# Two attentions on TensorE: the values of the item two back move ahead of the turns of the last item

## The reference

```python
s_w = jnp.einsum("bqgrd,bkgd->bgrqk", qb, kw) * scale
p_w = masked_softmax(s_w, mask_w)
o_w = jnp.einsum("bgrqk,bkgd->bqgrd", p_w, vw)
...
o = gb[..., 0:1] * o_c + gb[..., 1:2] * o_s + gb[..., 2:3] * o_w
```

```python
sc = (jnp.einsum('bchd,bicjhd->bhcij', q_row, k_win).astype(jnp.float32)
      + bias.astype(jnp.float32)[None])
p = jax.nn.softmax(sc.reshape(bsz, nh, GRID_W, win_r * NA_WIN_COLS), axis=-1)
...
return jnp.einsum('bhcij,bicjhd->bchd', p, v_win)
```

## Time and profile before

| what | value |
|---|---|
| median of 3 runs | 1695.55 us (1694.1 to 1696.63) |
| the profiled execution | 1696.4 us |
| its span, first to last instruction | 1694.7 us |
| mean granted TensorE clock | 0.999 |
| TensorE busy | 1661.1 us (98%) |
| DVE, ACT, POOL busy | 616.4, 664.9, 736.8 us |

### The profile page before, as it was taken

The page is one execution under the profiler, slowest core; times in us unless marked ns, Lnnn a source line. Parts: engine busy times, 40 slices in busy tenths (PEclk is TensorE's granted clock), DMA queues, the critical chain, the costliest instruction groups (busy, mean ns, idle before and its releaser), DMA issues. The chain is left out here.

```text
span 1694.7 us, 23049 instructions
## 1 busy us (share of the span) xinstructions
PE 1661.1 (98%) x8890; PEld 1335.7 (79%) x8890; DVE 616.4 (36%) x1156; ACT 664.9 (39%) x1013; POOL 736.8 (43%) x639
## 2 busy tenths in 40 slices
PE   9999999999999999999999999999999999999999
PEld 7777778877779888888878786767788888888887
DVE  5431865433242111011147343544556331212131
ACT  5223577454353432212245434434553441323130
POOL 5223343463144444644525544333355354544543
PEclk9999999999999999999999999999999999999999
DMA  5243101441033243433222234212264223232321
GB/s 181 75 149 97 63 29 55 143 142 58 26 99 100 76 124 100 145 96 82 99 77 75 100 108 141 85 56 90 68 210 161 86 81 110 83 100 99 100 100 50
DMA packets 152945, 166.09 MB, mean 98 GB/s; under 512 B 11959, under 2 KB 114434, under 8 KB 152835
## 3 DMA queue, kind: packets, MB, share of 16 engines
q1 hardware_dynamic: 145232, 151.20, 27.8%
q10 hardware_dynamic: 7602, 13.41, 2.2%
HBM read 155.68 MB, written 9.30 MB: 97 GB/s over the span
## 5 line engine op out<-in xcount | busy, mean ns | idle before, releaser
L807 POOL TENSOR_TENSOR w_low<-raw,w_high 128x512 fp32r<-128x512 f32 x501 | 668.5, 1368 | 845.1 <-ACT w_high L952 844.5
L952 ACT CAST w_high<-raw 128x2048 fp32r<-128x2048 f32 x127 | 239.0, 1882 | 234.0 <-PE bank L2321 221.1
L2326 PE MATMUL bank<-xT_high,w_high 128*128 128x512 f32 (+1 forms) x672 | 248.2, 375 | 0.0
L2327 PE MATMUL bank<-xT_low,w_high 128*128 128x512 f32 (+1 forms) x672 | 247.7, 374 | 0.0
L2315 PE MATMUL bank<-w_high,hid_high 128*128 128x512 f32 x432 | 168.4, 390 | 0.0
L2316 PE MATMUL bank<-w_high,hid_low 128*128 128x512 f32 x432 | 168.1, 389 | 0.0
L2330 PE MATMUL bank<-xT_high,w_low 128*128 128x512 f32 (+1 forms) x672 | 156.4, 374 | 0.7 <-POOL w_low L807 0.7
L2213 PE MATMUL bank<-xT_high,w_high 128*128 128x512 f32 (+1 forms) x360 | 150.4, 418 | 0.5 <-DVE share L2095 0.3
L2326 PEld LDWEIGHTS bank<-xT_high,w_high 128*128 128x128 f32 x672 | 126.5, 188 | 22.3
L2327 PEld LDWEIGHTS bank<-xT_low,w_high 128*128 128x128 f32 x672 | 126.5, 188 | 22.3
L2215 PE MATMUL bank<-xT_high,w_low 128*128 128x512 f32 (+1 forms) x360 | 141.0, 392 | 0.0
(11 more groups left out here) (433 smaller groups left out, 2564.6 us busy)
## 6 DMA issues: line engine op xcount, KB each, us to landing
raw<-in_w_in SPq DMA_DIRECT2D x33, 1024.0 KB, 5.1
raw<-in_w_down SPq DMA_DIRECT2D x26, 1024.0 KB, 5.0
raw<-in_w_gate_up SPq DMA_DIRECT2D x44, 512.0 KB, 5.0
raw<-in_w_up SPq DMA_DIRECT2D x16, 1024.0 KB, 5.3
raw<-in_w_kv_x SPq DMA_DIRECT2D x8, 1024.0 KB, 5.5
raw<-in_w_out SPq DMA_DIRECT2D x8, 1024.0 KB, 5.2
gate_dram<-qbuf ACTq DMA_DIRECT2D x20, 256.0 KB, 2.0
sg<-gate_dram ACTq DMA_DIRECT2D x6, 768.0 KB, 4.7
```

The source lines that it names most:

```text
L807: ins = pool.tensor_tensor(low[:, cs], full[:, cs], high[:, cs], ALU.subtract)
L952: own.tell(act.copy(split_slot(c, wh), split_slot(c, raw)), wh_done)
L2326: pe.matmul(ps[:, t0:t1], ch[:, k, cs], xh[:, k, t0:t1], start=q == 0, stop=False)
L2327: pe.matmul(ps[:, t0:t1], ch[:, k, cs], xl[:, k, t0:t1], start=False, stop=False)
```

## The change

In both loops the block of the values is moved ahead of the block of the turns, unchanged in itself: within a step TensorE now runs the scores, the dense pieces, the values of the item (or pair) two back and then the turns of the last one. Waits move with their instructions, and the fillers of steps 8 and 9 with the turns in which they stand. No other engine's program changes.

```diff
--- before.py
+++ after.py
@@ -2484,17 +2484,6 @@
                 if s == KX_STEP:
                     low_all("mem")
                 x_pieces(item_pieces(s))
-                if 1 <= s <= len(ITEMS):
-                    i = s - 1
-                    k = ITEMS[i][0] + 1
-                    for g, evac_sem in ((0, pt_a), (1, pt_v)):
-                        pe.wait_ge(s_exp, 2 * i + g + 1)
-                        if g == 1 and s in (8, 9):
-                            pe.wait_ge(o_taken, 1)
-                            keep_warm(15 - s, bank[2])
-                        if i:
-                            pe.wait_ge(evac_sem, i)
-                        transpose_blocks(TB[g], prob[:, i % 2, g, :], k).then_inc(pt_done, 1)
                 if s >= 2:
                     i = s - 2
                     qt, br, t = ITEMS[i]
@@ -2513,6 +2502,17 @@
                                                kvn[:, k, 256 * br + P + HD * g:256 * br + P + HD * g + HD],
                                                start=k == 0, stop=k == qt)
                     mm.then_inc(pv_done, 1)
+                if 1 <= s <= len(ITEMS):
+                    i = s - 1
+                    k = ITEMS[i][0] + 1
+                    for g, evac_sem in ((0, pt_a), (1, pt_v)):
+                        pe.wait_ge(s_exp, 2 * i + g + 1)
+                        if g == 1 and s in (8, 9):
+                            pe.wait_ge(o_taken, 1)
+                            keep_warm(15 - s, bank[2])
+                        if i:
+                            pe.wait_ge(evac_sem, i)
+                        transpose_blocks(TB[g], prob[:, i % 2, g, :], k).then_inc(pt_done, 1)
                 if s == SUM_STEP:
                     pe.wait_ge(s_taken, 2 * s + 2)
                     keep_warm(5, SB[0])
@@ -2786,13 +2786,6 @@
                     gate_pieces(window_piece(g), A_N[g])
                 if g == 0:
                     window_scores(1)
-                if 1 <= g <= pairs:
-                    i = g - 1
-                    w = 2 * item_keys(2 * i)
-                    pe.wait_ge(a_exp, 2 * i + 2)
-                    if i >= 2:
-                        pe.wait_ge((a_pta, a_ptv)[i % 2], i // 2)
-                    transpose_blocks(TB[i % 2], nprob[:, i % 2, :], w // P).then_inc(a_tr, 1)
                 if g >= 2:
                     i = g - 2
                     w = item_keys(2 * i)
@@ -2802,6 +2795,13 @@
                         evacuated(pe, c.tiles[k][0])
                     window_values(2 * i, nprobT[:, i % 2, 0:w])
                     window_values(2 * i + 1, nprobT[:, i % 2, w:2 * w]).then_inc(a_out, 1)
+                if 1 <= g <= pairs:
+                    i = g - 1
+                    w = 2 * item_keys(2 * i)
+                    pe.wait_ge(a_exp, 2 * i + 2)
+                    if i >= 2:
+                        pe.wait_ge((a_pta, a_ptv)[i % 2], i // 2)
+                    transpose_blocks(TB[i % 2], nprob[:, i % 2, :], w // P).then_inc(a_tr, 1)
             for j in range(ST):
                 gate_pieces(turn_piece(0) + 4 * j, 4)
                 turn("hm", j)
```

## The result

The changed kernel takes **1711.02 us** (median of 4 runs, 1710.39 to 1711.89), the kernel before beside it 1696.09 us (median of 4): 1.009 of before, 95% interval 1.0074 to 1.0106. The forecast was 1706.2 us. Direction and most of the size are as forecast; the time lies 4.8 us above the forecast and just above the upper end of the range. Of the 4.8 us, 0.5 are the kernel before, which took 1695.55 us when the forecast was made; against the kernel before beside it, the change costs 14.9 us where 10.6 were added up.

What follows compares the result with a forecast made beforehand. TensorE, busy 98% of the span, bounds the kernel. Causal 5.2 plus neighbourhood 5.35 us made 10.6 us on the profiled 1696.4 us, 1707.0; against the median, 1706.2 us. Range 1700 to 1711 us, held at 58%.

Steps and rivals of the forecast that it cites:

- the clock: Rival, 6%: TensorE idle in causal steps 8 and 9 drops to half clock, up to 2 to 4 us more, 1708 to 1711 us.
- Seams: New neighbours on TensorE cost 0.14 us in each of 36 steps of both attentions, 5.0 us in all.
- seams free: Rival, 12%: the new neighbours cost nothing and only waits remain, 5.6 us, 1701.2 us.
- Waits hidden: Rival, 12%: copies come early enough or VectorE's gapless run shortens; only the price of new neighbours remains, 5.0 us, 1700.6 us.
- faster: Rival, 4%: values fill the time in which turns wait, 2.5 us in four places; 1693.0 us, or 1698 us.
- nothing measurable: Rival, 8%: both terms a third of what was priced, or waits counted twice; 1696 to 1699 us.
- Steps 8 and 9: Causal attention: values wait for VectorE's late copies, fillers no longer cover; step 10's scores 2.5 us later, 0.84 of it seams.
- The 0.4 us more that I allowed for step 10: Causal attention: possible addition of 0.4 us because the turns of item 9 come later within step 10.
- Steps 13 to 31: Causal attention: copies end before the dense pieces, so only new neighbours cost, 19 x 0.14 = 2.7 us.
- Neighbourhood attention: New neighbours in 11 steps, 1.5 us, plus four places where a wait grows: 5.35 us, bounds 1.5 and 7.
- Step 2: Neighbourhood attention: the first values stand ahead of turns and wait for ACT's copy, about 0.3 us.
- step 4: Neighbourhood attention: dense pieces wait for a PSUM bank that ACT empties later, 0.6 us.

Runs made afterwards that it cites:

- warm_all: Changed kernel with filler matmuls in every idle wait that the new order made or left in the two attentions: 1706.52 us, ratio 1.0067.
- causal_only: Kernel before with values ahead of turns in the causal attention alone, neighbourhood attention in the old order: 1702.60 us, ratio 1.0042.
- steps_8_12: Kernel before with values ahead of turns only in steps 8 to 12 of the causal attention: 1700.28 us, ratio 1.0024.
- late_steps: Kernel before with values ahead of turns only from step 13 of the causal attention on: 1700.09 us, ratio 1.0023.
- fill_mid: Kernel before with only the neighbourhood attention in the new order, plus fillers ahead of waits in its steps 10 and 11: 1701.81 us, ratio 1.0032.
- fill_tail: Kernel before with only the neighbourhood attention in the new order, plus fillers ahead of waits in its last two steps: 1704.17 us, ratio 1.0039.

## Why the prediction missed

**The step that failed is the clock.** I had it in the sum at nothing, and as a rival of 6%, in steps 8 and 9 alone, at 2 to 4 us. It was in both profiles of the changed kernel, worth 4.35 us in the first and 4.4 us in the second (there the attentions grow by 7.58 and 6.98 us, in warm_all by 4.64 and 5.53; 1.6 of the 4.4 us come from the fall at 140 us, behind a wait that the change left alone), and not bound to the place that I gave it. Two slips made it: I counted as candidates only the two longest idle times (2.4 and 1.9 us), though the row that I had for a fall of the clock stood behind waits of 0.75 and 0.73 us; and I asked at which one place the clock would fall, where the question was how many such places the new order makes (eight waits of 0.57 to 1.89 us in the two attentions are new or longer) in a kernel whose mean clock was 0.999 or 1.000 in 51 of 70 executions. With the 4.35 us the forecast would have read 1710.6 us.

**Seams** (forecast 0.14 us a step): right. 0.127 us a step where they stand alone, 0.15 in the step shown, and with them the rival "seams free" is out. "Waits hidden" and "faster" are out by the rows above, "nothing measurable" by the result.

**Steps 8 and 9** (forecast S(10) 2.5 us later): right in its mechanism, too large in size, 1.70 us. The term at fault is VectorE's copy: I let it slip by 0.8 us, because the copy of T(3) comes later. That one does, 173.46 against 172.26 us, but the copies of T(6) and T(7) come 0.36 and 0.35 us later than before, no more than the first scores. VectorE still works without a gap in between; single pieces of its convolution are shorter, the one shown 0.48 us instead of 1.20 and another 0.83 instead of 0.99. My rival "waits hidden" had named this, VectorE's run falling otherwise against GpSimd's; it came true for 0.84 us. That GpSimd is the cause was not tried: its subtraction beside these pieces does begin 1.50 us later than before (189.37 against 187.87 us), but it already runs when the 0.48 us piece starts. Two things in the traces speak for GpSimd all the same. In the kernel before, the two pieces at L1662 take 1.68 and 1.65 us in step 7, beside GpSimd's subtractions, and 0.75 us each in step 8, when GpSimd is idle. And the piece shown takes 0.48 or 0.49 us in the three profiles where the seams stand ahead of it (after, causal_only, warm_all), 1.20 to 1.22 in three where they don't (before, steps_8_12, late_steps). So the 0.84 us of the seams ahead had no place in the sum. The 0.4 us more that I allowed for step 10 came: S(12) stands 0.51 us later still.

**Steps 13 to 31** (2.7 us): 2.42. Causal attention together 4.63 against 5.2.

**Neighbourhood attention** (5.35 us): 5.5 without the clock. Step 2 waits 0.19 us (forecast 0.3), step 4 0.71 us for ACT's move out of the bank (0.6), V(8) 0.71 (0.85), the pieces of step 11 0.93 instead of 0.34, so 0.59 more (0.6), the tail 1.6 (1.5); what is left, some 1.7 us over 11 seams, is their price (1.5).

**The sum** of 10.6 us is what warm_all measures with the clock held up, 11.0, and what the two profiles show without it, 10.1.

**What stays open** is why one execution drops its clock at one wait and another at the next: fill_mid kept full clock behind waits at which three other profiles lost it. The runs show that fillers in a wait keep the clock up behind it, and that the kernels with the new waits left open run at a lower mean clock; they don't show a rule for a single wait.

## What to carry to other kernels

When a change puts new idle waits on a TensorE that was busy throughout, price each twice, once as the wait and once as a chance of half clock behind it (here 1.4 to 1.5 us in step 11; at the end 1.4 to 1.5 us in three profiles and 3.0 in one), and look for the waits in the whole stretch and not only for the longest. Filler matmuls that stand between two parts of work are cover: check what they stood beneath before moving the part in front of them. And a swap of two blocks that moves no work may still cost a tenth of a microsecond at each step, if it puts neighbours of another kind beside each other.

## What the runs showed of the hardware

Waits as short as 0.71 and 0.93 us (steps 10 and 11), with matmuls between them, were followed by a granted clock of 0.50 (1.2 GHz instead of 2.4), during which pieces of 128x512 started 0.43 us apart instead of 0.23 (after, 1212.16 to 1212.59 us; fill_tail, 1232.13 to 1232.36). I had not expected falls behind so short waits, nor that the places change from one execution of the same program to the next while its time hardly does (1710.39 to 1712.24 us over eight). The Trainium skill has a case of this kind, "TensorE: Matmul & The Clock Gate", section "A second HAM failure mode: psum-queue depth-cycling", where brief idle times between groups of matmuls make the clock go back and forth; the traces here agree, with the numbers above.
